# A hybrid encoder layer on eight cores: projections, GpSimd sums, output tiles and first loads rearranged

## The chip, the cores and the metric

The kernel runs on the 8 cores of one Trainium2 chip. Each core computes its own slice of the batch and exchanges nothing with the others; all read the same weights from HBM. A time is the device time of the slowest core, in microseconds (us). TensorE (PE) multiplies; VectorE (DVE), ScalarE (ACT) and GpSimd (POOL) work elementwise; SyncE (SP) only issues DMAs, and GpSimd issues those that convert float32 to bfloat16 on the way.

## The reference

One layer, applied to 4 prompts of 4096 tokens and 16 samples of 32 tokens, with 1024 features:

```
x = x + 0.5 * SwiGLU_1(RMSNorm(x))                     # 1024 -> 2 x 2816 -> 1024
h = RMSNorm(x)
u, q, k, v, ga, gb = split(h @ w_in)                   # 512 | 1024 | 128 | 128 | 1024 | 1024
q, k = RMSNorm per head;  16 heads of 64, 2 KV heads
A = (pool(u, windows 2/4/8/16) - u) @ w_group * scale + bias ... @ w_pool_proj
B = attention over the own 64-token chunk and two before, with sinks ... @ w_attn_proj
x = x + (sigmoid(ga) * A + sigmoid(gb) * B) @ w_out
x = x + 0.5 * SwiGLU_2(RMSNorm(x))
```

It also returns the last pooling inputs (`o_pool_p`, `o_pool_s`) and the last K and V rows.

## The kernel before, in words

A core has 2240 token columns: 128 of halo, 2048 of a prompt, 64 of two samples. They lie in 5 groups `X[0]`..`X[4]` of 448 columns, features on partitions, as 8 tiles (kc or m) of 128 features. Group 0 has only 320 columns after the first feed-forward, since the halo falls away. `hT` holds the normed activations in bf16, for matmuls. Nearly all matmuls are 128x128 by 448 columns. In the profiled names `ring` is a buffer of 7 weight blocks, which GpSimd's queue fills from `wst` (`pump`); a block is loaded when an earlier one is released.

The instruction order on every engine is the order of the Python calls: `Prog` puts each operation on its engine's list and adds the semaphore waits that its reads and writes ask for. A DMA takes the next of its queue's semaphores (12 for SP, 12 for GpSimd), and so waits until the DMA 12 before it on that queue has landed. `P.guard()` is the last operation so far on each compute engine; an operation with `extra=mguard` waits for these.

Stages, with the core's times in the profile:

- **First feed-forward** (0 to 537). A norm is `norm_sq`: ScalarE squares tile kc of a group, TensorE adds the eight squares over the partitions with a matmul by a constant (L448), `norm_fin` takes ln and exp on ScalarE (L457, L459) into one of two `rstd` buffers, and VectorE multiplies X by it into `hT` (L462); these eight products wait in `hq`, and `drain(k)` issues k of them. `lagq` holds the constant matmuls; `tick(k)` issues all but the last k. `gate_multi` multiplies hidden blocks j for one group (L505); two blocks at once are interleaved kc by kc. `first_pass1` orders the first four blocks, during the loads. `out_proj` (L566) adds the result to X on VectorE (L570), and in its last pass also squares for the next norm, n2.
- **Projections** (537 to 657). For g in 0..4, `seq` calls K, V, the pool inputs U(0..3) and the queries Q(0..7). Each is followed by `next_step`, which drains products and issues the later parts of earlier steps: K and Q need `stat_mm` (a constant matmul L676 into the one bank 7, then ln and exp L678/L680 into an `rstd` buffer), U(c) has window sums on GpSimd (c + 1 adds, L750 to L757) and then a VectorE product into `ya` (L791). `kT`, `Vb` and the sample tiles `ksT`, `Vs` are cleared by GpSimd first (L621, L622, L848). V's copy (L727) carries `mguard`.
- **Attention with branch A** (657 to 797). 32 attention units, each scores (L923), exp, values (L966), a normed output in a tile `yt` (L986), and a DMA transpose of that tile into `qT` on SP's queue (L991). There are two such tiles in turn. Between them run gate (L1010) and projection (L1023) of branch A; the product into `mT[g]` (L1028) overwrites memory of X, `ub`, `ktm` and `vtm`. For the samples, `u_fin` sums and `u_last` finishes `ya`.
- **Branch B** (797 to 912), then **the mix output** (912 to 977): 5 groups x 8 tiles of 8 matmuls (L1106), X on VectorE (L1108), squares (L444) and constant matmuls (L448) for the norm n3.
- **Second feed-forward** (977 to the end), whose last pass sends X to `y_out` two tiles at a time.

## Time and profile before

| | us |
|---|---|
| median of 3 runs (1451.29 to 1614.0) | 1452.57 |
| the profiled execution | 1451.66 |
| its span, first to last instruction, slowest core (core 0) | 1450.6 |
| the other cores' spans | 1445.1 to 1449.7 |
| granted TensorE clock, every core | 1.000 |
| TensorE busy in the span | 1419.3 |
| VectorE, ScalarE, GpSimd busy | 608.4, 391.4, 139.3 |

The span is what the trace shows; the profiled execution's own time is 1.06 us more, for what lies before the first and behind the last instruction. Busy time of TensorE is the union of its matmuls, so a matmul that overlaps the one before it counts once. The "idle before" of an instruction is in square brackets in the timeline, with what ended it.

### The profile page before, as it was taken

To read this page: it belongs to the slowest core of one execution; us is meant where nothing else is said; L and a number is where in the kernel's file an instruction comes from. 1 tells how busy PE (TensorE), PEld (TensorE's weight loads), DVE (VectorE), ACT (ScalarE), POOL (GpSimd) and SP (SyncE) were. 2 spreads that over 40 slices of the span, in tenths; PEclk is the share of its full clock that TensorE was granted. 3 is DMA by queue.
4 is the path that set the end of the run, shared out by engine and by line. 5 is a ranking of instruction groups with operands and counts; after the bars stand their busy time and mean duration, and the time that the engine had idled before them with its cause. 6 is when DMAs were issued, how large, how long until landed. Compare 5 with 4: busy or idle time off the path is not lost.

```text
span 1450.6 us, 23849 instructions; the slowest of 8 cores (1445.1 to 1450.6 us)
## 1 busy us (share of the span) xinstructions
PE 1419.3 (98%) x8189; PEld 777.2 (54%) x8189; DVE 608.4 (42%) x1159; ACT 391.4 (27%) x640; POOL 139.3 (10%) x214
## 2 busy tenths in 40 slices
PE   5999999999999999998999999999999999999999
PEld 2555555555555455555666555555555555555554
DVE  3436226223422485565555344563252251253235
ACT  5620110111011356556554222442101101101110
POOL 2010000000000045561000000000000000000000
PEclk9999999999999999999999999999999999999999
DMA  9743410321011341226434812224404204200014
GB/s 227 173 66 49 72 31 15 51 52 30 1 30 30 93 191 27 25 31 106 67 67 59 247 30 44 66 47 78 79 2 73 45 1 73 45 1 1 1 37 203
DMA packets 61172, 93.04 MB, mean 64 GB/s; under 512 B 42912, under 2 KB 44512, under 8 KB 59776
## 3 DMA queue, kind: packets, MB, share of 16 engines
q0 software_dynamic: 17936, 57.32, 22.4%
q1 hardware_dynamic: 43120, 34.20, 8.0%
q8 instruction: 69, 1.13, 0.3%
q14 instruction: 47, 0.39, 0.1%
HBM read 114.97 MB, written 18.38 MB: 92 GB/s over the span
## 4 chain that ended last, share of the span: by engine, by line
PE 89%; DMA 3%; SPq 2%; issue 2%; DVE 2%; POOL 1%; ACT 1%; DVEq 0%; POOLq 0%; ACTq 0%
PE ps L505 44%; PE ps L566 22%; PE ps L1085 4%; PE ps L1090 4%; PE ps L1106 4%; PE ps L1010 2%; PE ps L836 2%; DMA qT<-yt 2%; PE ps L448 1%; PE ps L771 1%; PE ps L1023 1%; PE ps L923 1%; PE ps L966 1%; SPq L700 1%; DMA X<-xin 1%
## 5 line engine op out<-in xcount | busy, mean ns | idle before, releaser
L505 PE MATMUL ps<-hT,ring 128*128 128x448 bf16 (+1 forms) x3520 | 651.1, 348 | 4.2 <-DVE hT L462 3.9
L505 PEld LDWEIGHTS ps<-hT,ring 128*128 128x128 bf16 x3520 | 344.5, 98 | 308.8 <-issue 7.8
L519 DVE TENSOR_TENSOR Abuf<-ps,sl 128x448 bf16<-128x448 f32 (+1 forms) x220 | 134.0, 611 | 481.1 <-PE ps L505 463.8
L566 PE MATMUL ps<-Abuf,Wo 128*128 128x448 bf16 (+1 forms) x1760 | 330.9, 347 | 0.0
L518 ACT ACTIVATE sl<-ps 128x448 bf16<-128x448 f32 (+1 forms) x220 | 116.7, 533 | 727.1 <-PE ps L505 720.2
L566 PEld LDWEIGHTS ps<-Abuf,Wo 128*128 128x128 bf16 x1760 | 172.2, 98 | 151.1
L570 DVE SCALAR_TENSOR_TENSOR X<-ps,X 128x448 f32<-128x448 f32 (+1 forms) x320 | 195.5, 611 | 114.9 <-PE ps L566 113.4
L394 POOL DMA_DIRECT2D ring<-wst x71 | 38.2, 539 | 903.6 <-PE ps L505 608.3
L462 DVE SCALAR_TENSOR_TENSOR hT<-X,colv,rstd 128x448 bf16<-128x448 f32 (+1 forms) x120 | 76.6, 669 | 37.9 <-ACT rstd L459 37.9
L1010 PE MATMUL ps<-hT,ring 128*128 128x448 bf16 (+1 forms) x320 | 63.7, 342 | 0.1
L1085 PE MATMUL ps<-hT,ring 128*128 128x448 bf16 (+1 forms) x320 | 63.6, 342 | 0.0
L1090 PE MATMUL ps<-qT,ring 128*128 128x448 bf16 (+1 forms) x320 | 63.6, 342 | 0.0
L1106 PE MATMUL ps<-mT,ring 128*128 128x448 bf16 (+1 forms) x320 | 63.1, 342 | 0.0
L444 ACT ACTIVATE sq<-X 128x448 bf16<-128x448 f32 (+1 forms) x80 | 45.2, 565 | 64.7 <-DVE X L1108 37.8
L836 PE MATMUL ps<-hT,ring 128*128 128x448 bf16 (+1 forms) x320 | 61.5, 342 | 0.0
L929 ACT ACTIVATE PT<-ps,colv 128x1536 bf16<-128x1536 f32 (+2 forms) x34 | 49.8, 1466 | 42.3 <-DVE yt L986 24.4
L1092 DVE SCALAR_TENSOR_TENSOR pb<-tb,ps 128x448 f32<-128x448 f32 (+1 forms) x40 | 23.8, 595 | 63.0 <-PE ps L1090 61.3
L1087 ACT ACTIVATE tb<-ps,hbg 128x448 f32<-128x448 f32 (+1 forms) x40 | 24.5, 613 | 89.0 <-DVE mT L1094 55.1
L1085 PEld LDWEIGHTS ps<-hT,ring 128*128 128x128 bf16 x320 | 31.3, 98 | 25.8
L1090 PEld LDWEIGHTS ps<-qT,ring 128*128 128x128 bf16 x320 | 31.3, 98 | 25.8
L1106 PEld LDWEIGHTS ps<-mT,ring 128*128 128x128 bf16 x320 | 31.3, 98 | 25.7
L836 PEld LDWEIGHTS ps<-hT,ring 128*128 128x128 bf16 x320 | 31.1, 98 | 25.6 <-issue 0.3
(104 smaller groups left out, 803.4 us busy)
## 6 DMA issues: line engine op xcount, KB each, us to landing
ring<-wst POOLq DMA_DIRECT2D x63, 512.0 KB, 6.3
Wo<-wo POOLq DMA_DIRECT2D x12, 768.0 KB, 9.9
xsp<-X SPq DMA_DIRECT2D x5, 1792.0 KB, 6.1
X<-xsp SPq DMA_DIRECT2D x5, 1792.0 KB, 17.6
X<-xin POOLq DMA_DIRECT2D x8, 896.0 KB, 29.9
y_out<-X SPq DMA_DIRECT2D x6, 896.0 KB, 3.6
ring<-wst POOLq DMA_DIRECT2D x8, 384.0 KB, 10.0
Wo<-wo POOLq DMA_DIRECT2D x4, 512.0 KB, 5.6
```

The lines of the kernel that those rows point to most:

```text
L462: P.dve(lambda: V.scalar_tensor_tensor(out=hT[:, kc, C0[g] + lo:C0[g] + lo + n], in0=X[g][:, kc, lo:lo + n], scalar=cv_[:, gcol + kc:gcol ...
L505: P.pe(lambda: T.matmul(ps[:, bks[x][half], 0:n], lhsT=w[:, kc, 128 * half:128 * half + 128], rhs=hT[:, kc, c0s[g]:c0s[g] + n], start=(kc ...
L518: P.act(lambda: S.activation(out=slt[i][:, 0:n], in_=ps[:, bg, 0:n], func=AF.Silu), r=[bank[bg]], w=[r_sl[i]])
L519: P.dve(lambda: V.tensor_tensor(out=Abuf[:, jj, c0s[g]:c0s[g] + n], in0=ps[:, bu, 0:n], in1=slt[i][:, 0:n], op=ALU.mult), r=[bank[bu], r_s ...
L566: P.pe(lambda: T.matmul(ps[:, bk, 0:n], lhsT=Wo[b][:, jj, 128 * m:128 * m + 128], rhs=Abuf[:, jj, c0s[g]:c0s[g] + n], start=(jj == 0), sto ...
L570: P.dve(lambda: V.scalar_tensor_tensor(out=X[g][:, m, lo[g]:lo[g] + n], in0=ps[:, bk, 0:n], scalar=0.5, in1=X[g][:, m, lo[g]:lo[g] + n], o ...
L836: P.pe(lambda: T.matmul(ps[:, bk, 0:n], lhsT=w[:, kc, 128 * (m % 2):128 * (m % 2) + 128], rhs=hT[:, kc, c0:c0 + n], start=(kc == 0), stop= ...
L929: P.act(lambda: S.activation(out=pt[:, a:z, :], in_=ps[:, a:z, :], func=AF.Exp, scale=0.125, bias=cv_[:, col:col + 1]), r=[bank[x] for x i ...
L1010: P.pe(lambda: T.matmul(ps[:, gb, 0:n], lhsT=w[:, kc, :], rhs=hT[:, kc, c0:c0 + n], start=(kc == 0), stop=(kc == KC - 1)), r=rw + [rh[g][k ...
L1085: P.pe(lambda: T.matmul(ps[:, bg, 0:n], lhsT=w[:, kc, :], rhs=hT[:, kc, c0:c0 + n], start=(kc == 0), stop=(kc == KC - 1)), r=rw + [rh[g][k ...
L1090: P.pe(lambda: T.matmul(ps[:, bp, 0:n], lhsT=w[:, 8 + x, :], rhs=qT[:, mm0 // 64:(mm0 + n) // 64, x, :], start=(x == 0), stop=(x == 7)), r ...
L1106: P.pe(lambda: T.matmul(ps[:, bk, 0:n], lhsT=w[:, c, 128 * (m % 2):128 * (m % 2) + 128], rhs=mT[g][:, c, :], start=(c == 0), stop=(c == 7) ...
```

## The change

- SP's queue gets 24 DMA semaphores. Group 0's four load pieces go from GpSimd's queue to SP's. GpSimd's weight loads wait for the first of the pieces.
- `first_pass1` runs blocks 0 and 1 of group 0 together and finishes group 0's four blocks before group 1's.
- In the last pass of `out_proj` before a norm, the drain behind tile 4 is left out. The last group's n2 norm has an `rstd` buffer of its own, `rst2`. `next_step` drains one product instead of two. Group 0's pool inputs are taken in the order 0, 1, 2, 3.
- For n3, GpSimd adds the squares of tiles 0 to 6 (six adds a group, into `accL` and at last into a bf16 tile), and TensorE runs two constant matmuls a group instead of eight, behind the first output tile of the next group.
- The pooling outputs go from SP's queue to GpSimd's. The loads into `ksT` and `Vs` have a resource for each half. `yt` gets a third tile. `u_last` of 3 and 2 moves into the last group's last two steps, that of 1 and 0 behind the first `mT` product.
- The last output tile of the last group is computed and sent in two halves of 224 columns, tile 6 by itself.

```diff
+    accB, e = at("accB", [128, GW], BF16, mend)
+    e = scr + NSQ * 2 * GW
+    accL, e = at("accL", [128, GW], F32, e)
+    accM, e = at("accM", [128, GW], BF16, e)
...
-    P = Prog(nc)
+    P = Prog(nc, {"sp": 24, "pool": 12})
...
-    yts, r_yts = [yt, yt2], [R("yt"), R("yt2")]
+    yts, r_yts = [yt, yt2, yt3], [R("yt"), R("yt2"), R("yt3")]
+    al_y = [r_sq[2:4], [], r_rst[1:2]]
...
+    r_us, r_kn = R("usT"), R("kns")
+    r_ks, r_vs = [R("ksT0"), R("ksT1")], [R("Vs0"), R("Vs1")]
...
-            P.dma("pool", lambda: nc.gpsimd.dma_start(out=ring[:, 2048 * sl_:2048 * sl_ + w_], in_=wst[i, :, 0:w_]), w=[r_ring[sl_]])
+            P.dma("pool", lambda: nc.gpsimd.dma_start(out=ring[:, 2048 * sl_:2048 * sl_ + w_], in_=wst[i, :, 0:w_]), w=[r_ring[sl_]], extra=x0[0:1])
...
-    load_x(0, 2)
+    x0 = [P.dma("sp", lambda a=a: nc.sync.dma_start(out=X[0][:, a:a + 2, :], in_=xin[:, 0, a:a + 2, :]), w=rX[0][a:a + 2])
+          for a in range(0, KC, 2)]
     pump_to(2)
     load_x(1, 4)
     pump_to(4)
...
-        lagq.append(mm)
+        if key != "n3":
+            lagq.append(mm)
+            return
+        ac, rac = accL, r_sl[0:2]
+        ab, rab = (accB, r_accB) if g % 2 == 0 else (accM, r_sl[2])
+        if kc == 0:
+            sqp[g] = (t, rt)
+        elif kc < KC - 1:
+            src, rsrc = (sqp[g][0], [sqp[g][1]]) if kc == 1 else (ac, rac)
+            dst, rdst = (ab, [rab]) if kc == KC - 2 else (ac, rac)
+            P.gps(lambda: G.tensor_tensor(out=dst[:, 0:n], in0=src[:, 0:n], in1=t[:, 0:n], op=ALU.add), r=rsrc + [rt], w=rdst,
+                  extra=ng_["sq"])
+        else:
+            def mm2():
+                P.pe(lambda: T.matmul(ps[:, sbk, 0:n], lhsT=cb[:, 0, :], rhs=ab[:, 0:n], start=True, stop=False),
+                     r=[rab, r_cb], w=[bank[sbk]])
+                P.pe(lambda: T.matmul(ps[:, sbk, 0:n], lhsT=cb[:, 0, :], rhs=t[:, 0:n], start=False, stop=True),
+                     r=[rt, r_cb], w=[bank[sbk]])
+                norm_fin(key, g, lo, n, gcol, sbk)
+            lagq.append(mm2)
...
+        if key == "n2" and g == NG - 1:
+            rs, rrs = rst2, r_rst2
+        else:
+            i = cnt["rst"] % 2
+            cnt["rst"] += 1
+            rs, rrs = rst[i], r_rst[i]
...
             feed(0)
             tick(0)
             drain(8)
-            gate_multi([(0, 0)], 0, True)
+            post = gate_multi([(0, 0), (1, 1)], 0, post=False)
             feed(1)
-            post = gate_multi([(1, 1)], 0, post=False)
             tick(0)
-            drain(8)
+            drain(3)
             post()
+            drain(3)
             gate_multi([(2, 2)], 0)
-            feed(2)
-            gate_multi([(0, 0), (1, 1)], 1)
-            gate_multi([(2, 2)], 1)
+            drain(2)
             gate_multi([(3, 3)], 0)
-            tick(0)
-            drain(8)
...
             for m in range(KC):
                 bk = nb(FB6 if last and gcol_next is not None else FB)
-                for jj in range(len(js)):
-                    P.pe(lambda: T.matmul(ps[:, bk, 0:n], lhsT=Wo[b][:, jj, 128 * m:128 * m + 128],
-                                          rhs=Abuf[:, jj, c0s[g]:c0s[g] + n], start=(jj == 0), stop=(jj == len(js) - 1)),
-                         r=[r_Wo[b], r_A[jj][g]], w=[bank[bk]], sig=(jj == len(js) - 1))
+                end = last and store and g == NG - 1 and m == KC - 1
                 rx_ = [rX[g][m]]
-                P.dve(lambda: V.scalar_tensor_tensor(out=X[g][:, m, lo[g]:lo[g] + n], in0=ps[:, bk, 0:n], scalar=0.5,
-                                                     in1=X[g][:, m, lo[g]:lo[g] + n], op0=ALU.mult, op1=ALU.add),
-                      r=[bank[bk]] + rx_, w=rx_)
-                drain(1)
+                for (a, z) in ([(0, n // 2), (n // 2, n)] if end else [(0, n)]):
+                    if a:
+                        bk = nb(FB)
+                    for jj in range(len(js)):
+                        P.pe(lambda: T.matmul(ps[:, bk, 0:z - a], lhsT=Wo[b][:, jj, 128 * m:128 * m + 128],
+                                              rhs=Abuf[:, jj, c0s[g] + a:c0s[g] + z], start=(jj == 0), stop=(jj == len(js) - 1)),
+                             r=[r_Wo[b], r_A[jj][g]], w=[bank[bk]], sig=(jj == len(js) - 1))
+                    wx_ = [R("end%d" % a)] if end else rx_
+                    P.dve(lambda: V.scalar_tensor_tensor(out=X[g][:, m, lo[g] + a:lo[g] + z], in0=ps[:, bk, 0:z - a], scalar=0.5,
+                                                         in1=X[g][:, m, lo[g] + a:lo[g] + z], op0=ALU.mult, op1=ALU.add),
+                          r=[bank[bk]] + rx_, w=wx_)
+                    if end:
+                        out_dmas.append(P.dma("sp", lambda: nc.sync.dma_start(
+                            out=y_out[:, g, m:m + 1, lo[g] + a:lo[g] + z], in_=X[g][:, m:m + 1, lo[g] + a:lo[g] + z]), r=wx_))
+                if not (last and gcol_next is not None and m == 4):
+                    drain(1)
                 if last and gcol_next is not None:
                     norm_sq(next_key, g, m, lo[g], n, gcol_next)
                 tick(2)
                 if last and store:
-                    step = 2 if g == NG - 1 else 4
-                    if m % step == step - 1:
+                    step = 4 if g < NG - 1 else 2 if m < 6 else 1
+                    if m % step == step - 1 and not end:
                         a = m - step + 1
                         out_dmas.append(P.dma("sp", lambda a=a, m=m, g=g: nc.sync.dma_start(
...
         sched["t"] += 1
         tick(0)
-        drain(2)
+        drain(1)
...
         if cg == 3:
-            out_dmas.append(P.dma("sp", lambda: nc.sync.dma_start(out=o_pool_p, in_=b[:, :, o - 16:o]), r=rbs))
-            out_dmas.append(P.dma("sp", lambda: nc.sync.dma_start(out=o_pool_s, in_=b[:, :, o:o + 64]), r=rbs))
+            out_dmas.append(P.dma("pool", lambda: nc.gpsimd.dma_start(out=o_pool_p, in_=b[:, :, o - 16:o]), r=rbs))
+            out_dmas.append(P.dma("pool", lambda: nc.gpsimd.dma_start(out=o_pool_s, in_=b[:, :, o:o + 64]), r=rbs))
...
         for p in range(2):
             P.dma("pool", lambda p=p: nc.gpsimd.dma_start(
-                out=ksT[64 * p:64 * p + 64, :, :, :, p, :].rearrange("k s h c q -> k (s h c) q"), in_=ckT), w=[r_ks])
+                out=ksT[64 * p:64 * p + 64, :, :, :, p, :].rearrange("k s h c q -> k (s h c) q"), in_=ckT), w=[r_ks[p]])
             P.dma("pool", lambda p=p: nc.gpsimd.dma_start(
-                out=Vs[64 * p:64 * p + 64, :, :, :, p, 0:64].rearrange("k s c h d -> k (s c h) d"), in_=cvT), w=[r_vs])
+                out=Vs[64 * p:64 * p + 64, :, :, :, p, 0:64].rearrange("k s c h d -> k (s c h) d"), in_=cvT), w=[r_vs[p]])
...
-        def Q(m, yc=None, uf=None):
+        def Q(m, yc=None, uf=None, ul=None):
             def f():
+                if ul is not None:
+                    u_last[ul]()
...
-        if g < NG - 1:
+        if g == 0:
+            seq = [K, Vv(0, 1, 2, 3), U(0), Q(0), Q(1), U(1), Q(2, 3), Q(3), U(2), Q(4, 2), Q(5), U(3), Q(6, 1), Q(7, 0)]
+        elif g < NG - 1:
             seq = [K, Vv(0, 1, 2, 3), U(3), Q(0), Q(1), U(2), Q(2, 3), Q(3), U(1), Q(4, 2), Q(5), U(0), Q(6, 1), Q(7, 0)]
         else:
-            seq = [U(3), K, U(2), Vv(0, 1, 2, 3), U(1), Q(0), U(0), Q(1, None, 3), Q(2, 3, 2), Q(3, 2, 1), Q(4, 1, 0), Q(5, 0), Q(6), Q(7)]
+            seq = [U(3), K, U(2), Vv(0, 1, 2, 3), U(1), Q(0), U(0), Q(1, None, 3), Q(2, 3, 2), Q(3, 2, 1), Q(4, 1, 0), Q(5, 0), Q(6, None, None, 3), Q(7, None, None, 2)]
...
-        k = ucnt["y"] % 2
+        k = ucnt["y"] % 3
         ucnt["y"] += 1
         yo, ryo = yts[k], r_yts[k]
         for h in range(2):
...
-                  r=[bank[3 + h], r_dn2[h]], w=[ryo] + ([] if k else al_yt))
+                  r=[bank[3 + h], r_dn2[h]], w=[ryo] + al_y[k])
...
-    turn = [[], [(3, 4), (2, 1)], [(1, 4), (0, 3)]]
+    turn = [[], [(3, 4), (2, 6)], [(1, 4), (0, 3)]]
...
+            a_mul(c, g, pbn)
             if ai == 0:
-                for x in (3, 2, 1, 0):
-                    u_last[x]()
-            a_mul(c, g, pbn)
+                u_last[1]()
+                u_last[0]()
             if ai < len(turn):
...
             drain(1)
+            tick(0)
             norm_sq("n3", g, m, lo_, n, C_G3)
-            tick(2)
```

How the change moves instructions at three places. Names: `X_44` to `X_48` are groups 0 to 4, `mT_120`/`mT_125` is group 0's mix input and `mT_86`/`mT_87` group 1's, `vtm` V's copy, `ub` a pool input, `ktm` K's result, `sq` a tile of squares, `cb` the constants; rows give line, operation, tiles, size, and how often in a row.

VectorE, from the last output tiles of the first feed-forward into the first projections, before:

```order
L462 SCALAR_TENSOR_TENSOR hT<-X_47,colv,rstd_64 128x448
L570 SCALAR_TENSOR_TENSOR X_48<-ps,X_48 128x448
L462 SCALAR_TENSOR_TENSOR hT<-X_47,colv,rstd_64 128x448 x3
L462 SCALAR_TENSOR_TENSOR hT<-X_48,colv,rstd_64 128x448 x2
L727 CAST vtm_97<-ps 128x384
L729 CAST vtm_97<-ps 64x128
L462 SCALAR_TENSOR_TENSOR hT<-X_48,colv,rstd_64 128x448 x2
L775 COPY ub_95<-ps 128x336
L462 SCALAR_TENSOR_TENSOR hT<-X_48,colv,rstd_64 128x448 x2
L696 SCALAR_TENSOR_TENSOR ktm_96<-ps,colv,rstd_65 128x448
```

and now:

```order
L607 SCALAR_TENSOR_TENSOR X_48<-ps,X_48 128x448 x2
L499 SCALAR_TENSOR_TENSOR hT<-X_46,colv,rstd_65 128x448
L607 SCALAR_TENSOR_TENSOR X_48<-ps,X_48 128x448
L499 SCALAR_TENSOR_TENSOR hT<-X_47,colv,rstd_64 128x448
L607 SCALAR_TENSOR_TENSOR X_48<-ps,X_48 128x448
L499 SCALAR_TENSOR_TENSOR hT<-X_47,colv,rstd_64 128x448 x7
L499 SCALAR_TENSOR_TENSOR hT<-X_48,colv,rst_101 128x448
L768 CAST vtm_98<-ps 128x384
L770 CAST vtm_98<-ps 64x128
L499 SCALAR_TENSOR_TENSOR hT<-X_48,colv,rst_101 128x448
L816 COPY ub_96<-ps 128x336
```

Seven products of group 3 stand behind the last output tile where three stood, and the last product of group 2 stands two output tiles from the end, where it stood six from it; those of group 4 come one at a time.

TensorE, the first groups of the mix output, before:

```order
L1106 MATMUL ps<-mT_120,ring 128x320 x24
L448 MATMUL ps<-sq_57,cb 128x320
L1106 MATMUL ps<-mT_120,ring 128x320 x8
L448 MATMUL ps<-sq_58,cb 128x320
L1106 MATMUL ps<-mT_120,ring 128x320 x8
L448 MATMUL ps<-sq_59,cb 128x320
```

and now:

```order
L1151 MATMUL ps<-mT_125,ring 128x320 x64
L1151 MATMUL ps<-mT_87,ring 128x448 x8
L480 MATMUL ps<-accB,cb 128x320
L482 MATMUL ps<-sq_60,cb 128x320
L1151 MATMUL ps<-mT_87,ring 128x448 x56
```

A constant matmul stood behind every output tile; now two stand behind the first tile of the next group, of which the first reads what GpSimd's last add wrote.

GpSimd's queue at the start, before:

```order
L381 DMA X_44<-xin 128x896 x4
L394 DMA ring<-wst 128x2048 x2
L381 DMA X_45<-xin 128x1792 x2
L394 DMA ring<-wst 128x2048 x2
L381 DMA X_46<-xin 128x1792 x2
```

and now:

```order
L406 DMA ring<-wst 128x2048 x2
L393 DMA X_45<-xin 128x1792 x2
L406 DMA ring<-wst 128x2048 x2
L393 DMA X_46<-xin 128x1792 x2
L393 DMA X_47<-xin 128x1792 x2
```

The four pieces of group 0 left this queue; the rest kept its order.

## Rows read from the trace of the kernel before

**Rows 1.** The page's head and part 1, busy time by engine, its first line.

```profile
span 1450.6 us, 23849 instructions; the slowest of 8 cores (1445.1 to 1450.6 us)
...
PE 1419.3 (98%) x8189; PEld 777.2 (54%) x8189; DVE 608.4 (42%) x1159; ACT 391.4 (27%) x640; POOL 139.3 (10%) x214
```

**Rows 2.** Busy time by stretch: length, then each engine's, clock, DMA share, GB/s.

```profile
0.00:60.00 60.00, 43.76 (x204) 20.14 (x205) 21.25 (x40) 34.14 (x57) 11.77 (x25) 1.00 0.91 221
...
480.00:540.00 60.00, 59.15 (x329) 31.00 (x327) 44.00 (x74) 30.12 (x52) 16.60 (x5) 1.00 0.38 144
540.00:600.00 60.00, 55.25 (x370) 32.60 (x368) 32.96 (x60) 35.42 (x69) 34.28 (x49) 1.00 0.28 47
...
660.00:800.00 140.00, 134.19 (x1091) 89.40 (x1090) 73.85 (x260) 76.31 (x80) 5.18 (x12) 1.00 0.44 71
...
914.00:978.00 64.00, 64.00 (x360) 35.04 (x359) 40.12 (x69) 28.82 (x51) 2.83 (x5) 1.00 0.26 62
```

**Rows 3.** Timeline of the start: start, duration, engine, line, operation, [idle before].

```profile
1.06 0.40 SPq L377 DMA_DIRECT2D colv<-colv  x1
...
1.57 2.30 POOL L381 DMA_DIRECT2D X<-xin  x4 [0.87 <-POOLq L158]
...
13.62 1.04 ACT L444 ACTIVATE sqx<-X 128x448 bf16<-128x448 f32 x2 [1.15 <-DMA X<-xin]
...
16.67 0.53 POOL L394 DMA_DIRECT2D ring<-wst  x1 [2.06 <-DMA ring<-wst]
...
17.92 7.63 PE L505 MATMUL ps<-hT,ring 128*128 128x448 bf16 x32 [2.58 <-DVE hT L462]
...
19.88 0.71 POOL L492 DMA_DIRECT2D Wo<-wo  x1 [2.67 <-DMA ring<-wst]
...
36.58 1.98 ACT L444 ACTIVATE sqx<-X 128x448 bf16<-128x448 f32 x4 [0.34 <-DMA X<-xin]
...
50.23 6.21 PE L505 MATMUL ps<-hT,ring 128*128 128x448 bf16 x32 [0.65 <-DVE hT L462]
```

**Rows 4.** DMA issues of the page: count, KB each, median us to landing.

```profile
y_out<-X SPq DMA_DIRECT2D x4, 448.0 KB, 2.5
...
colv<-colv SPq DMA_DIRECT2D x1, 80.0 KB, 2.0
```

**Rows 5.** Timeline of the projections' start and of the sample set-up.

```profile
530.39 7.69 POOL L622 MEMSET Vb<- 128x9100 bf16 x1 [3.02 <-ACT sq L444]
...
538.19 0.93 POOL L624 MEMSET Vb<- 64x70 bf16 x2
...
542.05 0.55 DVE L727 CAST vtm<-ps 128x384 bf16<-128x384 f32 x1
...
544.52 1.27 DVE L462 SCALAR_TENSOR_TENSOR hT<-X,colv,rstd 128x448 bf16<-128x448 f32 x2
...
544.81 1.58 POOL L750 TENSOR_TENSOR S<-ub 128x335 f32<-128x335 f32 x1 [5.68 <-DVE ub L775]
...
547.15 0.30 PE L676 MATMUL ps<-sq,cb 128*128 128x320 bf16 x1 [1.51 <-ACT rstd L678]
...
550.61 0.87 DVE L791 SCALAR_TENSOR_TENSOR ya<-S,ub 128x320 bf16<-128x320 f32 x1 [2.62 <-POOL S L789]
...
591.12 0.68 POOL L857 DMA_DIRECT2D ksT<-ckT  x1 [3.52 <-DMA Vs<-cvT]
```

**Rows 6.** Timeline of the attention's start.

```profile
662.92 0.35 PE L825 MATMUL ps<-ya,Wpw 128*128 128x448 bf16 x1 [1.32 <-DVE mT L1028]
...
673.16 0.62 DVE L1028 SCALAR_TENSOR_TENSOR mT<-tg,ps 128x448 bf16<-128x448 f32 x1 [5.44 <-DMA o_pool_s<-ub]
```

**Rows 7.** Groups by shape: GpSimd's adds; VectorE's products within 914 to 978.

```profile
L753 POOL TENSOR_TENSOR S<-S 128x461 f32<-128x461 f32 x9 | 8.6, 955 | 1.3
...
L462 DVE SCALAR_TENSOR_TENSOR hT<-X,colv,rstd 128x448 bf16<-128x448 f32 x22 | 14.9, 677 | 0.7 <-ACT rstd L459 0.7
```

**Rows 8.** Timeline of one square in the mix output, and of the last output tile.

```profile
929.35 0.58 ACT L444 ACTIVATE sq<-X 128x448 bf16<-128x448 f32 x1 [0.90 <-DVE X L1108]
...
1447.19 0.62 DVE L570 SCALAR_TENSOR_TENSOR X<-ps,X 128x448 f32<-128x448 f32 x1 [0.51 <-PE ps L566]
```

43 lines of the change are left out of this document (23 added, 20 removed).

## Prediction

> **What bounds the kernel now.** I read the views in this order. The page's first part: TensorE is busy in 1419.3 of 1450.6 us, and no other engine in half of it [rows 1]. So there are two ways to gain: matmuls that go away, and the 31.3 us in which TensorE idles. The table of stretches says where these are: 16.2 us in the first 60, 0.9 in 480 to 540, 4.8 in 540 to 600, 5.8 in 660 to 800; what is left, 3.6 us, lies behind the last matmul [rows 2]. Everywhere else TensorE is full, and work of other engines is free as long as nobody waits for it. The timeline of each such stretch then names the wait [rows 3, 5, 6]. A 448-column matmul costs (6.21 - 0.16) / 32 = 0.189 us (32 in 6.21, of which 0.16 is the last one's overlap) [rows 3]; one of 320 columns 320/448 of it, 0.135.
>
> The sum is made against the profiled execution, 1451.66 us; the median shown is 0.9 us higher.
>
> **Start.** Today group 0's last piece is squared at 13.62, TensorE's first gate matmul runs 4.3 us later, at 17.92, weight blocks 0 and 1 have landed at 16.67 and 19.88 (GpSimd waits for them to reuse their semaphores), and the second half of group 2 at 36.58 [rows 3]. From 13.62 to 36.58 landed four blocks (128 x 2048 x 4 bytes, 1.05 MB each) and two groups (1.84 MB each), 7.87 MB in 23.0 us, 343 KB/us. Group 0's four blocks in the new order need the same amount: groups 0 and 1, blocks 0 to 3. A DMA of SP issued at 1.06 landed 2.0 us later [rows 3, 4], so the stream runs from about 3.1, and I add 1.0 for the hold, in which SP's pieces run alone: block 3 lands at 3.1 + 23.0 + 1.0 = 27.1. Behind it stand its 16 matmuls (3.0) and, for group 1, 32 gate matmuls, 8 constant ones and 32 more (13.6): group 2's first gate matmul at 43.7, today 50.23 [rows 3]. **-6.5 us.** The pairing itself gives four matmuls per product of VectorE (0.76 against 0.61 us), where two were not enough, but the landing covers this. Ends: if SP's pieces come no faster than GpSimd's did, the stream is only shifted by the queue's earlier first byte, about 1.5 us: block 3 at 13.6 + 6.03/0.343 - 1.5 = 29.7, so -3.9. If only TensorE counted, group 0 landing at 8.5 (3.1 + 1.84/0.343), first matmul at 12.8, then 144 matmuls (27.2): 40.0, -10. The row on the rate is the nearest to both, so I stay with the value in between.
>
> The Trainium skill ("DMA: Bandwidth & Descriptors", Issuing engines are not separate DMA queues) says that all queues share the same 16 DMA engines, so another queue gives no more bandwidth. By it the gain is in the first byte alone, the -3.9 end. No row here shows both queues loading at once at the start.
>
> **Last pass before n2, and projections.** Today TensorE waits 1.5 us at 547.15 and 1.8 at 552.70 for an `rstd` buffer; behind the first stands VectorE, whose product of K comes late behind pairs of group 4's products, behind the second VectorE again, held 2.62 us by GpSimd's chain for U(3), which is slowed to 1.58 us for a 335-column add beside VectorE's products [rows 5]. `rst2`, one drain a step and U(0) first (one add) take both causes away. But the skipped drains leave seven products of group 3 for the end, and the last product of group 2 now comes four output tiles later (4 x 1.33 us). GpSimd's clearing of `Vb` writes over group 2 and waits for it: it began at 530.39 and ended, with the two small ones, at 539.1 [rows 5]; it will end at about 544.3. V's copy carries `mguard` and ran at 542.05 [rows 5], so VectorE's queue now stands until 544.3. Behind it: copies 0.9, product 0.6, copy 0.5, product 0.6, K's product 0.6, and so on to the first query's product at 550.7; that query's `rstd` buffer is needed for the third query's ln, and the fourth's constant matmul, wanted at 549.5, waits for bank 7 until about 551.3. I put 1.9 us of wait in the place of 3.3: **-1.4**. Ends: 0 and -3.3, as the wait for the clearing is covered or not.
>
> At 591.12 GpSimd had waited 3.52 us for the first half of `Vs` before it could issue the second, and the window sums behind it came late; of that 1.4 us reached TensorE (4.75 in 540 to 600, less the two above) [rows 2, 5]. With a resource per half the wait is gone: **-1.4**, nothing late behind it.
>
> **Attention.** At 673.16 VectorE had stood 5.44 us for `o_pool_s`, issued last on a congested SP queue; TensorE lost 2.2 of it. At 662.92 TensorE waited 1.3 us for bank 1 behind eight small `ya` products [rows 6]. On GpSimd's queue the two outputs are issued near 651, behind two weight loads, and have until 669 to land; they push GpSimd's sample sums by about 1.4 us (two issues of 0.7, as the one at 591.12 [rows 5]), which VectorE's slack there takes. -2.2, and -0.8 for the bank, since `mT`, the last four `ya` products and bank 4 still come in a row. The other 2.2 us of the stretch [rows 2] are spread over six places where `yt` waits for the transpose that reads it; a third tile adds a unit's time, 3.6 us, and I take 1.9 of it. Sum **-4.9**, ends -2.5 (the pooling outputs land late behind the weight loads) and -5.8.
>
> **Mix output.** The stretch 914 to 978 is full [rows 2]. Six constant matmuls a group go: 4 x 6 x 0.189 + 6 x 0.135 = -5.3 us. What is put in: six GpSimd adds a group, one per output tile (8 x 0.189 = 1.51 us). An f32 add of 461 columns takes 0.955 [rows 7], 448 columns 0.93. Beside VectorE it is slower: the 335-column add would take 0.73 by columns and took 1.58, while about 1.1 us of products ran [rows 5], so it lost 0.75 of the overlap. A product takes 0.68 in each 1.51 [rows 7]: add 0.93 + 0.75 x 0.68 = 1.43, with a gap of 0.13 it is 1.56 a tile. From the end of tile 1's matmuls: X 0.62 and square 0.58 [rows 8] and three hand-overs of some 0.15 give 1.65; six adds end at 1.65 + 5 x 1.56 + 1.43 = 10.9. TensorE wants the sum behind tile 0 of the next group, seven tiles later, at 10.6. So 0.4 us of wait with the hand-over, in four groups (the fifth has 16 matmuls of the next stage as cover): +1.5. Net **-3.8**, ends -5.3 (the adds keep 0.93) and -0.1 (next paragraph). The fewer matmuls make the tile 1.51 instead of 1.70 us; VectorE needs 1.30 of it.
>
> The Trainium skill ("SBUF — State Buffer", Who interferes with whom) says that a VectorE instruction with two SBUF inputs and a GpSimd instruction that reads SBUF exclude each other wholly. The row shows three quarters of the overlap lost, not all.
>
> **Tail.** The last X operation starts at 1447.19, takes 0.62, and its DMA of 448 KB lands about 2.5 later [rows 4, 8]. A half tile takes some 0.39 on VectorE and 112 KB land nearer to the 2.0 of the small load [rows 4]: **-0.7**, ends -0.2 and -1.2. The 0.9 us in 480 to 540 stay.
>
> Sum: -6.5 - 1.4 - 1.4 - 4.9 - 3.8 - 0.7 = -18.7, so 1433.0 us.
>
> **Rivals.**
> - *The adds are fully locked out.* Then an add is 0.93 + 0.68 = 1.61, with the gap 1.74 a tile; six end at 1.65 + 8.7 + 1.61 + 0.1 = 12.1, 1.5 us late in three groups beside full-width products, 0.9 in the one beside 320-column ones: +5.4 in place of +1.5, 1437 us. For it: the adds are slowed at all; against: the 1.58. This is what the skill's rule would do.
> - *The start gains only the first byte*: -3.9 in place of -6.5, 1435.5 us. With the lock-out as well, 1439.5.
> - *The clearing of `Vb` and the late outputs cost what they were to save*: projections at -1.4 together, attention at -2.5: 1437 us.
> - *Slower than before.* The sum on GpSimd becomes TensorE's bound. The adds read bf16, and no row has an add of two bf16 tiles. With a us a tile, a sum is 6a - 8.8 late; the other gains and the matmuls make 20.2 us, so over four groups it turns at 6a = 13.9, a = 2.3 us, 2.4 times today's 0.955. At 2.5 us: 1451.7 - 20.2 + 4 x 6.2 = 1456. Against: the slowest 335-column row scales to 2.1 us at 448 columns, and there products ran for 70% of the time.
> - *It does not do what it says*: the third tile or the early transfer changes nothing, as SP's congestion between 650 and 670 stays; that is inside the ends above.
>
> **Chances and range.** A measurement of this kernel tells about 2% (29 us) from no change. The forecast with its terms near their values, 1428 to 1436: 0.55. Rivals that leave 1436 to 1441, alone or two together: 0.27. Better than 1428, more terms at their good ends (all of them give 1425): 0.10. Above 1441: 0.08, of it 0.03 above 1452. Range 1427 to 1441. Over 2% faster means under 1423.5, beyond all good ends together: 0.02. Over 2% slower asks for adds of 3.5 us: 0.02. Within 2%: 0.96.
>
> **What would show it.** Group 2's first gate matmul at 43 to 45 us; blocks 0 and 1 landed by 16. A VectorE wait of about 2 us before V's copy, released by the clearing of `Vb`, and one wait of about 2 us of TensorE before 552. No GpSimd wait in the sample set-up. No wait of `mT` for `o_pool_s`, no wait of `yt` for a transpose. In the mix output, GpSimd adds of 1.3 to 1.5 us and waits of under 0.6 us before four of the new constant matmuls. The forecast is wrong if these adds take over 1.7 us, or if the landing of the first blocks is not earlier than today.

## The result and the profile after

The changed kernel takes 1435.49 us (median of 1435.44 to 1435.60), the kernel before took 1451.29 and 1452.57: a ratio of 0.9884, interval 0.9865 to 0.9904. Executions in which the cores of a die ran long at a lower granted clock are left out, here and in every time below. The forecast was 1433.0, the range 1427 to 1441. The total held; how it is made up did not.

The page's head and its first line of busy time, after:

```profile
span 1434.4 us, 23887 instructions; the slowest of 8 cores (1432.7 to 1434.4 us)
...
PE 1413.2 (99%) x8165; PEld 775.7 (54%) x8165; DVE 616.3 (43%) x1160; ACT 388.6 (27%) x638; POOL 168.9 (12%) x242
```

Against [rows 1] TensorE now idles 21.2 us, not 31.3. The stretches that answer to [rows 2] (length, then each engine's busy time, clock, DMA share, GB/s):

```profile
0.00:60.00 60.00, 45.53 (x211) 21.48 (x212) 21.53 (x41) 32.68 (x57) 9.55 (x21) 1.00 0.90 221
540.00:600.00 60.00, 58.06 (x378) 33.88 (x376) 35.63 (x65) 37.17 (x71) 41.21 (x56) 1.00 0.26 38
660.00:800.00 140.00, 139.12 (x1125) 93.15 (x1126) 74.88 (x256) 75.83 (x81) 5.15 (x12) 1.00 0.49 81
914.00:978.00 64.00, 63.98 (x347) 33.74 (x346) 52.17 (x76) 29.71 (x50) 27.85 (x29) 1.00 0.29 61
```

The idle time of 540 to 800 is nearly gone; that of the start (14.5 us) is not. VectorE is 12 us busier in the last stretch, but that stretch now holds 18 us of the second feed-forward. In the mix output by itself VectorE is busy 48.0 us, before 40.7 (core 0), with one product a tile as before. These 7 us will matter below.

Idle time in a window says little once the windows hold different work. So I cut both traces at the same matmuls (the first output matmul, the first of the projections, the first gate matmul of branch A, the first of branch B, of the mix output, of the second feed-forward, and the last) and took the median of the eight cores for each piece, in us:

| piece | before | after | measured | forecast |
|---|---|---|---|---|
| start to first output matmul | 104.71 | 102.57 | -2.1 | -6.5 |
| projections | 118.78 | 117.02 | -1.8 | -2.8 |
| attention with branch A | 138.28 | 134.30 | -4.0 | -4.9 |
| branch B | 114.24 | 114.24 | 0 | 0 |
| mix output | 63.88 | 58.96 | -4.9 | -3.8 |
| behind the last matmul | 4.02 | 2.98 | -1.0 | -0.7 |

(The rest of the two feed-forwards takes 432.1 and 471.4 us before, 432.1 and 471.5 after.) These make 13.8 us, while the slowest core's span fell by 16.2. The difference is spread among the cores: attention took 136.8 to 140.4 us on the eight cores before and takes 134.3 to 134.5 now, and the time is that of the slowest core. Core 0, the slowest before, won 2.3, 2.9, 6.1, 0, 4.9 and 0.9 us in the six rows.

### The profile page after: what moved, and what is told of

Same layout as the page of the kernel before. It is cut to its first block, busy times and chain, and to the rows that moved or that the text cites. A ratio compares the mean times of both kernels' runs of the same rounds, so it can differ in the third digit from the quotient of the medians.

```text
span 1434.4 us, 23887 instructions; the slowest of 8 cores (1432.7 to 1434.4 us)
## 1 busy us (share of the span) xinstructions
PE 1413.2 (99%) x8165; PEld 775.7 (54%) x8165; DVE 616.3 (43%) x1160; ACT 388.6 (27%) x638; POOL 168.9 (12%) x242
## 4 chain that ended last, share of the span: by engine, by line
PE 98%; DMA 1%; issue 0%; DVE 0%; ACT 0%; POOL 0%; SPq 0%; DVEq 0%; ACTq 0%; POOLq 0%
PE ps L542 45%; PE ps L603 22%; PE ps L1055 4%; PE ps L1151 4%; PE ps L1135 4%; PE ps L1130 4%; PE ps L877 4%; PE ps L1068 2%; PE ps L812 2%; PE ps L1011 1%; PE ps L968 1%; PE ps L462 1%; DMA ring<-wst 1%; PE ps L763 1%; PE ps L717 1%; PE ps L731 1%
## 5 line engine op out<-in xcount | busy, mean ns | idle before, releaser
L603 PE MATMUL ps<-Abuf,Wo 128*128 128x448 bf16 (+2 forms) x1766 | 330.9, 346 | 0.0
L499 DVE SCALAR_TENSOR_TENSOR hT<-X,colv,rstd 128x448 bf16<-128x448 f32 (+1 forms) x112 | 79.5, 739 | 34.0 <-ACT rstd L496 34.0
L458 ACT ACTIVATE sq<-X 128x448 bf16<-128x448 f32 (+1 forms) x80 | 45.0, 564 | 57.6 <-DVE X L1153 30.7
L1151 PE MATMUL ps<-mT,ring 128*128 128x448 bf16 (+1 forms) x320 | 57.9, 342 | 0.0
L877 PEld LDWEIGHTS ps<-hT,ring 128*128 128x128 bf16 x320 | 31.1, 98 | 26.6 <-issue 1.2
L1135 PEld LDWEIGHTS ps<-qT,ring 128*128 128x128 bf16 x320 | 31.3, 98 | 25.8
L1130 PEld LDWEIGHTS ps<-hT,ring 128*128 128x128 bf16 x320 | 31.3, 98 | 25.8
L1151 PEld LDWEIGHTS ps<-mT,ring 128*128 128x128 bf16 x320 | 31.3, 98 | 25.2
```

The lines of the kernel that those rows point to most:

```text
L499: P.dve(lambda: V.scalar_tensor_tensor(out=hT[:, kc, C0[g] + lo:C0[g] + lo + n], in0=X[g][:, kc, lo:lo + n], scalar=cv_[:, gcol + kc:gcol ...
L603: P.pe(lambda: T.matmul(ps[:, bk, 0:z - a], lhsT=Wo[b][:, jj, 128 * m:128 * m + 128], rhs=Abuf[:, jj, c0s[g] + a:c0s[g] + z], start=(jj == ...
L877: P.pe(lambda: T.matmul(ps[:, bk, 0:n], lhsT=w[:, kc, 128 * (m % 2):128 * (m % 2) + 128], rhs=hT[:, kc, c0:c0 + n], start=(kc == 0), stop= ...
L1130: P.pe(lambda: T.matmul(ps[:, bg, 0:n], lhsT=w[:, kc, :], rhs=hT[:, kc, c0:c0 + n], start=(kc == 0), stop=(kc == KC - 1)), r=rw + [rh[g][k ...
L1135: P.pe(lambda: T.matmul(ps[:, bp, 0:n], lhsT=w[:, 8 + x, :], rhs=qT[:, mm0 // 64:(mm0 + n) // 64, x, :], start=(x == 0), stop=(x == 7)), r ...
L1151: P.pe(lambda: T.matmul(ps[:, bk, 0:n], lhsT=w[:, c, 128 * (m % 2):128 * (m % 2) + 128], rhs=mT[g][:, c, :], start=(c == 0), stop=(c == 7) ...
```

## The experiments

All are edits of the changed kernel, each compared on the same chip with the kernel before.

### The start

Its timeline after (start, duration, engine, line, operation, idle before and what ended it), against [rows 3]:

```profile
7.32 1.21 POOL L406 DMA_DIRECT2D ring<-wst  x2 [6.61 <-DMA X<-xin]
...
12.50 1.04 ACT L458 ACTIVATE sqx<-X 128x448 bf16<-128x448 f32 x2 [1.27 <-DMA X<-xin]
...
16.71 0.53 POOL L406 DMA_DIRECT2D ring<-wst  x1 [2.90 <-DMA ring<-wst]
16.80 0.90 PE L542 MATMUL ps<-hT,ring 128*128 128x448 bf16 x2 [2.58 <-DVE hT L499]
19.28 8.64 PE L542 MATMUL ps<-hT,ring 128*128 128x448 bf16 x30 [1.58 <-DMA ring<-wst]
...
27.76 1.68 PE L462 MATMUL ps<-sqx,cb 128*128 128x448 bf16 x8
...
29.27 12.27 PE L542 MATMUL ps<-hT,ring 128*128 128x448 bf16 x64
...
42.89 12.27 PE L542 MATMUL ps<-hT,ring 128*128 128x448 bf16 x64
```

Group 0's last piece comes 1.1 us earlier, blocks 0 and 1 no earlier at all. TensorE stops after two matmuls for block 1. Then 30 matmuls take 8.64 us: one by one, the first 15 of them start 0.373 us apart, the rest 0.189. 448 columns in 0.373 us are 1.2 GHz, the lower of the two levels, though the granted clock reads 1.00 in this stretch; ahead of them TensorE had run for 0.9 us in the last 5. On core 0 of the kernel before 8 gate matmuls were so slow; over the cores it is 8 to 16 before and 11 to 16 now. Group 2's first gate matmul is the 33rd of the last row, at 48.9 (48.1 on the median core), where 43.7 was forecast.

From 19.28 on TensorE has no pause in these rows. Block 3's first matmul is the 17th of the row at 29.27, at 32.3, while block 3 landed at 30.7. So it is on all eight cores: block 3's first matmul starts 0.5 to 1.6 us behind its landing, with no wait for it. What TensorE does wait for is block 1, 1.3 to 2.3 us.

**Undo the start, and undo the queue alone.** Both put group 0 back on GpSimd's queue; the first also restores the old order of blocks.

```diff
-    x0 = [P.dma("sp", lambda a=a: nc.sync.dma_start(out=X[0][:, a:a + 2, :], ...
+    load_x(0, 2)
...
-..., w=[r_ring[sl_]], extra=x0[0:1])
+..., w=[r_ring[sl_]])
```

> The changed kernel with its start undone: group 0's pieces on GpSimd's queue again, no hold, and the old order of the first blocks. My reading of the two traces: the start is worth the 2.3 us by which core 0's projections begin earlier, so 1437.9 us, group 2's first gate matmul back at 50.2 and that of the changed kernel at 48 to 49. The prediction's own term was 6.5: then 1442. If the start is worth nothing, 1435.6.

> The changed kernel with group 0's pieces on GpSimd's queue and no hold, but with the new order of the first blocks. From the start to the first output matmul lie 102.6 us in the changed kernel, 104.7 with the old start. If the order is what counts: 102.6 to 103, and SP's queue is worth little; if SP's queue is (its last piece lands 1.1 us earlier): 103.7 to 104, the end 1437.

Measured: 1439.12 us with the old start, 1437.06 with the new order on the old queue. The first piece of the kernel lasts 104.69 and 102.92 us, against 102.57. So the order of blocks is worth 1.8 us. The 0.35 of SP's queue can't be told from nothing: seven executions with the changed kernel's start (it, its repetition and five runs below that change later stages) gave 102.0 to 102.9 us for this piece. With SP's queue the first gate matmul starts 1.1 us earlier, at 16.2 for 17.3; TensorE then waits longer for block 1 (1.66 us for 1.02) and runs 14.5 slow matmuls in place of 12.5 (all medians), and the 1.1 us are spent. Both runs lost 0.8 us more in the mix output, 59.8 us for 59.0, on all cores, with not one instruction changed there; see below.

**Without the hold.**

```diff
-..., w=[r_ring[sl_]], extra=x0[0:1])
+..., w=[r_ring[sl_]])
```

> The changed kernel without GpSimd's wait for the first piece of group 0. Theory H (the hold cost the stream what SP's queue gained: block 3 landed at 30.74, before at 30.77): without it blocks 0 to 3 land 2.5 to 3.5 us earlier, the 1.6 us wait for block 1 goes, fewer gate matmuls run 0.373 us apart, and the end comes 2 to 3 us earlier, 1433 us. Rival (the two queues only share, and group 0's pieces are what TensorE needs first): the last piece lands 1.5 to 3 us later, the first gate matmul with it at 18.5 or later, blocks no use before: 1435.5 to 1437.

Measured: 1442.97 us, 7.5 slower than the changed kernel; the first piece takes 109.4 us, 6.8 more. Blocks 0 and 1 do land earlier, as the first theory has it (block 3 doesn't), and group 0 later, as the second has it, but by 9.6 us and not by 1.5 to 3; the first gate matmul starts at 25.7. The squares of group 0 in that run:

```profile
7.10 1.04 ACT L458 ACTIVATE sqx<-X 128x448 bf16<-128x448 f32 x2 [1.10 <-DMA X<-xin]
...
12.82 1.04 ACT L458 ACTIVATE sqx<-X 128x448 bf16<-128x448 f32 x2 [4.68 <-DMA X<-xin]
...
17.77 1.04 ACT L458 ACTIVATE sqx<-X 128x448 bf16<-128x448 f32 x2 [3.90 <-DMA X<-xin]
...
22.25 1.04 ACT L458 ACTIVATE sqx<-X 128x448 bf16<-128x448 f32 x2 [3.44 <-DMA X<-xin]
...
26.55 9.06 PE L542 MATMUL ps<-hT,ring 128*128 128x448 bf16 x32 [2.58 <-DVE hT L499]
```

Beside GpSimd's stream SP's pieces land 4 to 6 us apart; with GpSimd held until the first had landed they came 1.5 to 2.3 apart. Landings in us, medians of the cores:

| | group 0, last piece | block 0 | block 1 | block 3 |
|---|---|---|---|---|
| before | 12.9 | 16.0 | 18.9 | 30.7 |
| old start | 12.9 | 16.0 | 18.9 | 31.3 |
| new order, old queue | 13.0 | 16.0 | 19.1 | 30.9 |
| changed | 11.8 | 15.8 | 18.7 | 30.5 |
| without the hold | 21.4 | 11.5 | 16.1 | 31.1 |

Block 3 lands at 30.5 to 31.3 whatever the queue, the hold and the order of the first pieces. The forecast had 27.1. Why no order of these loads brings it earlier was not tested.

**Blocks 0 and 1 one after the other.**

```diff
-            post = gate_multi([(0, 0), (1, 1)], 0, post=False)
+            gate_multi([(0, 0)], 0, True)
             feed(1)
+            post = gate_multi([(1, 1)], 0, post=False)
```

> The changed kernel with blocks 0 and 1 of group 0 one after the other instead of interleaved. Theory P: the pairing made TensorE wait 1.6 us for block 1 at 17.7 and start again with slow matmuls, 17 at 0.373 us in place of 8; without it both go, 3 us on TensorE, of which blocks 2 and 3 (27.8 and 30.7) leave about 1: 1434.5 us. Rival: VectorE's products (0.61 us each for two matmuls) stretch the first block again and nothing is won: 1435.5.

Measured: 1435.33 us (1434.83 to 1435.53), first piece 102.08 us. The wait for block 1 is gone, and 10 matmuls are slow, not 14.5 (medians); but 102.08 lies within the 102.0 to 102.9 of equal starts, and the whole time tells nothing either.

**Zero matmuls to keep the clock up**, alone and with the blocks apart. `warm(k)` issues k matmuls of a cleared 448-column tile.

```diff
             feed(0)
-            tick(0)
+            warm(16)
+            for k in (6, 4, 8, 14):
+                tick(len(lagq) - 2)
+                warm(k)
             drain(8)
```

> The changed kernel with 48 extra matmuls of zeros on TensorE before the first gate matmul (16 ahead of the first constant one, then 6, 4, 8 and 14 behind its pairs), so that TensorE hardly idles between 2.5 and 16 us. Theory C: the 17 gate matmuls that ran 0.373 us apart ran at 1.2 GHz because TensorE had idled, and run 0.19 us apart here, worth 3.2 us on TensorE; as block 3 lands at 30.7 only 1.5 to 2 of them reach the end: 1433.8 us. Rival: the 0.373 comes from the late data or from the loads' traffic, not from the clock: the spacing stays, 1435.5.

> The changed kernel with blocks 0 and 1 one after the other and zero matmuls wherever TensorE would idle before 27 us (48 ahead of the first gate matmul, 20 ahead of group 1's constants). The landings (block 2 near 27.9, block 3 near 30.7) stay. Theory L (the landings bound the start, the slow matmuls and the wait for block 1 hide in front of them): block 3's matmuls end at 34.3 in place of 35, the first output matmul at 101.5 to 102 (102.1 with the blocks alone), the end at 1434.8 to 1435.3 us. Rival (the slow matmuls reach the end): 100.5 and 1433.7.

Measured: 1436.07 us alone, 1437.91 with both (and 20 zero matmuls ahead of group 1's constants). TensorE in the first of these runs, core 0:

```profile
16.82 0.54 PE L543 MATMUL ps<-hT,ring 128*128 128x448 bf16 x2
...
19.05 5.84 PE L543 MATMUL ps<-hT,ring 128*128 128x448 bf16 x30 [1.69 <-DMA ring<-wst]
...
26.40 1.75 PE L463 MATMUL ps<-sqx,cb 128*128 128x448 bf16 x4 [0.76 <-ACT sqx L459]
...
28.50 7.71 PE L543 MATMUL ps<-hT,ring 128*128 128x448 bf16 x31 [0.35 <-DMA ring<-wst]
```

The clock theory holds: 30 matmuls take 5.84 us, not 8.64, with the same loads under way. And it is worth nothing (first piece 102.75 us): TensorE then waits for group 1's squares and block 2, and after that nine matmuls are 0.373 apart again. Five of the eight cores have seven to nine such slow matmuls, three of them already behind the wait for block 1; three cores have none. The length of the pauses doesn't sort them: core 4 has none behind pauses of 2.26 and 1.60 us, core 3 has seven behind one of 1.85. With the long filler no core has a slow matmul, and TensorE pauses for 0.34 us in all between its first gate matmul and group 2's; it is no faster, since 20 x 0.189 = 3.8 us of zeros stand where the waits and the slow matmuls were (first piece 103.4 us). The slowest cores of that run also ended 5 us behind their last matmul, where 3 is usual; that is the larger part of its 1437.9 and I have no cause for it. The changed kernel run beside it took 1435.45.

> The changed kernel itself on the same chip, for the comparison: 1435.5 us.

**Block 2 ahead of group 1, and its queue mended.** The loads go W0, W1, W2, group 1, W3, and group 0's three blocks run before group 1's constants.

```diff
-    pump_to(2)
+    pump_to(3)
     load_x(1, 4)
...
             drain(8)
-            post = gate_multi([(0, 0), (1, 1)], 0, post=False)
+            gate_multi([(0, 0)], 0, True)
+            gate_multi([(1, 1)], 0, True)
+            post = gate_multi([(2, 2)], 0, True, post=False)
             feed(1)
             tick(0)
-            drain(3)
             post()
-            drain(3)
-            gate_multi([(2, 2)], 0)
-            drain(2)
+            drain(8)
             gate_multi([(3, 3)], 0)
```

The first of the two runs has zero matmuls besides.

> The changed kernel with block 2 loaded ahead of group 1 (landing some 21.5 us instead of 27.8), blocks 0, 1 and 2 of group 0 one after the other, then group 1's constant matmuls, then block 3, and with zero matmuls (48 ahead of the first gate matmul, 10 ahead of group 1's constants) so that TensorE's clock stays up. Blocks 0 to 3 of group 0 end when block 3 has landed (30.7) plus its 16 matmuls, at 33.7 instead of 35.3 to 36: first output matmul at 100 to 101 in place of 102.6, the end 1433.5 us. If group 1's pieces, now 2.5 us later, hold it up: 102.6, 1435.5.

> The same without the zero matmuls. If the slow gate matmuls hide behind the landing of block 3, as in the run with zero matmuls alone, this is as fast as its sister: 1433.5 us; if not, 1.5 us slower.

Measured: 1439.22 and 1438.71 us, first piece 105.5 and 104.8. VectorE's products of group 1 stood behind block 2's product, and that behind ScalarE's table loads (1.28 us each); TensorE idled 2.0 to 3.0 us ahead of group 1's first gate matmul, near 36. The second version puts `post()` between the halves of group 1's squares:

> As best_w, but block 2's silu between the two halves of group 1's squares and its product ahead of group 1's eight, since there VectorE's products stood behind that product and ScalarE's table loads (first gate matmul of group 1 at 35.8 us, 2 to 3 us of idle ahead of it). If that queue was all that was wrong, group 1's gates start at 33.5 to 34, the first output matmul comes at 101 to 101.5 (102.6 in the changed kernel), and the end at 1434 us. If the landings (block 2 at 21.6, group 1 at 27.2) leave nothing to win, 102.6 and 1435.5.

> The same without the zero matmuls: equal to its sister if the slow matmuls fit in the time until block 3 lands, 1434 us; 1435 if not.

Measured: 1436.06 and 1435.90 us, first piece 102.5 and 102.8.

**One piece of group 0 on SP's queue, the other three first on GpSimd's**, without the hold and with blocks 0 and 1 apart, then with the order just told:

> Only the first piece of group 0 on SP's queue, the other three first on GpSimd's, no hold, blocks 0 and 1 one after the other. Theory S (a queue's own start and the hold, not the bandwidth, set when the stream runs: in the changed kernel block 0 landed 3.8 us after group 0's last piece, before 2.6): the last piece lands at 11.5 to 12.5, block 0 near 14.5, block 1 near 17.5, block 3 near 29.5, the first output matmul at 101 to 101.5 us, the end at 1434. Rival (the sharing of the two queues delays the pieces, as without the hold, where the first gate matmul came at 25.7): first gate matmul after 17.5 and 1436 us or more.

> x_one's loads with b3_n's order of blocks: if both help, the first output matmul at 100 us and the end at 1433 us; if TensorE, and not the stream, is the bound by then, as x_one.

Measured: 1436.40 and 1437.07 us, first piece 102.55 and 103.4. Apart from the two with the blocked queue, the start of every variant with a new order of blocks and group 0 not starved lasts 102.1 to 103.4 us, and most of that is the spread of equal starts.

### The sums on GpSimd

```diff
-        if key != "n3":
+        if True:
             lagq.append(mm)
             return
...
-            tick(0)
             norm_sq("n3", g, m, lo_, n, C_G3)
+            tick(2)
```

> The changed kernel with the sums of n3 back on TensorE: eight constant matmuls a group, no GpSimd adds. Between the first matmul of the mix output and the first gate matmul of the second feed-forward lie 59.0 us in the changed kernel and 63.9 in the one before. Theory A (only the matmuls count, 24 x 0.189 + 6 x 0.135 = 5.3 us, less some waits): 63.9 us here, the end 4.9 later, 1440.4. The prediction's 3.8 would give 1439.3. Second theory, on who pays where both engines read SBUF: VectorE's products of this stage took 0.68 us before and 0.85 with the adds at 1.03; without the adds they take 0.68 again.

Measured: 1440.32 us; the mix output takes 63.88 us, as before. So the sums on GpSimd are worth 4.9 us, close to the 5.3 of the matmuls taken out; no wait came in their place. Groups by shape (count, busy, mean ns of one, idle before) of the changed kernel, GpSimd's adds on core 5 (895 to 978) and VectorE's products on core 0 (905 to 978, so some of the next stage's are among them):

```profile
L476 POOL TENSOR_TENSOR accL<-accL,sq 128x448 f32<-128x448 f32 x16 | 16.6, 1038 | 7.3 <-ACT sq L458 6.3 <-PE ps L1151 0.9
```

```profile
L499 DVE SCALAR_TENSOR_TENSOR hT<-X,colv,rstd 128x448 bf16<-128x448 f32 x32 | 26.9, 854 | 1.4 <-ACT rstd L496 1.4
```

and of the kernel with the sums on TensorE, core 0, the same stretch:

```profile
L499 DVE SCALAR_TENSOR_TENSOR hT<-X,colv,rstd 128x448 bf16<-128x448 f32 x32 | 21.3, 677 | 1.9 <-ACT rstd L496 1.9
```

The adds keep 1.04 us. It is VectorE's product that pays: 0.854 in place of 0.677, 5.6 us over these 32, all of it in slack. The forecast had GpSimd pay, at 1.43 an add.

Which of the two pays goes by which starts first. Group 1's first add in the changed kernel, core 0:

```profile
914.29 1.03 POOL L476 TENSOR_TENSOR accL<-sq,sq 128x448 f32<-128x448 bf16 x1 [4.26 <-ACT sq L458]
914.36 1.30 DVE L499 SCALAR_TENSOR_TENSOR hT<-X,colv,rstd 128x320 bf16<-128x320 f32 x1
```

and the same in the kernel with the old start, core 0, where everything up to here lies 3.50 us later:

```profile
917.86 0.54 DVE L498 SCALAR_TENSOR_TENSOR hT<-X,colv,rstd 128x320 bf16<-128x320 f32 x1
918.09 1.20 POOL L475 TENSOR_TENSOR accL<-sq,sq 128x448 f32<-128x448 bf16 x1 [4.56 <-ACT sq L457]
...
919.43 5.91 POOL L475 TENSOR_TENSOR accL<-accL,sq 128x448 f32<-128x448 f32 x4
925.49 1.37 POOL L475 TENSOR_TENSOR accM<-accL,sq 128x448 bf16<-128x448 f32 x1
```

Here the product starts 0.23 us ahead of the add and takes its 0.54; the add takes 1.20. From then on that chain of adds runs without a pause at 1.37 each, 1.5 apart, each behind a product's start, and TensorE waits 0.7 us for the sum. In the changed kernel the add started 0.07 us ahead, kept 1.03, and the product took 1.30. All cores agree. Take the pairs of a full-width add and a product that start within 0.4 us of each other, with no earlier add beside the product. In the changed kernel the add is first in all 24 of them: it keeps its 1.03 to within 0.01, and the product takes 0.48 to 0.76 us more. With the old start the product is first in 48 of 56: it keeps its 0.54, and the add takes 0.17 to 0.35 us more; in the other eight it is as in the changed kernel. The kernel with the new order on GpSimd's queue shows the same 48. So 0.3 us of start decide over 0.8 us of the end; what delayed the add in these two kernels the traces don't show. The Trainium skill ("SBUF — State Buffer", Who interferes with whom) says, of VectorE's two-port modes, that whoever issues first gets the shared ports for the whole instruction. The order agrees; but locked out wholly, the product would have taken 0.96 + 0.54 = 1.50, and it took 1.30.

**Every add twice.**

```diff
+            P.gps(lambda: G.tensor_tensor(out=ab[:, 0:n], in0=src[:, 0:n], in1=t[:, 0:n], op=ALU.add), ...
             P.gps(lambda: G.tensor_tensor(out=dst[:, 0:n], in0=src[:, 0:n], in1=t[:, 0:n], op=ALU.add), ...
```

> The changed kernel in which GpSimd does every add of the n3 sum twice, the extra one into the bf16 tile: 12 a group. By the prediction's formula a sum of six is 6a - 8.8 us late with a us a tile; with a = 2 x 1.04 = 2.1 that is 3.7 us in three groups and 0.7 in the first, 12 us in all: 1447.5 us, and more, up to 1456, if the adds then lie beside VectorE's products all the time and GpSimd is the one that is held up (a = 2.5). If VectorE pays instead, its products grow over 0.85 and the adds stay at 1.04: 1447.

Measured: 1475.17 us, 1.6% slower than the kernel before. TensorE's waits between 900 and 1000 (in total, times, longest), and its clock (third column from the end) by stretch, core 0, where the mix output lasts from 899.8 to 990.8:

```profile
PE ps L482 <- POOL accB L478: 16.5, 3, 7.1
PE ps L482 <- POOL accM L478: 12.6, 2, 6.6
```

```profile
900.00:930.00 30.00, 24.04 (x138) 13.61 (x136) 14.97 (x27) 10.54 (x19) 19.64 (x21) 0.94 0.27 80
930.00:960.00 30.00, 17.79 (x77) 8.47 (x78) 10.68 (x17) 7.39 (x13) 18.90 (x17) 0.74 0.00 1
...
992.00:1000.00 8.00, 3.00 (x16) 1.65 (x14) 1.44 (x3) 3.02 (x4) 7.41 (x9) 0.74 0.11 11
1000.00:1010.00 10.00, 10.00 (x51) 5.29 (x50) 6.59 (x11) 4.38 (x7) 0.76 (x2) 0.87 1.05 179
1010.00:1020.00 10.00, 10.00 (x55) 5.19 (x53) 1.87 (x3) 1.74 (x4) 0.56 (x1) 1.00 0.71 106
```

With 12 adds of about 1.2 us the queue never empties. By the prediction's formula a sum 6.6 us late means (6.6 + 8.8) / 6 = 2.6 us a tile. So the slower rival is real. At 2.6 us a tile its formula gives 4 x 6.6 = 26 us of waits in four groups; measured on core 0 are 24.1. Two things come on top. The fifth group waits too, 5.0 us, which the forecast held covered; this wait lies already in the next stage. And TensorE's clock falls once it pauses in every group: the granted clock has a mean of 0.74 in two of the stretches, between the levels of 1.2 and 2.4 GHz, and 38 matmuls of the mix output are 0.373 us apart, which costs about 7 us (some 9 on cores 3 and 5). The mix output takes 31.9 us more, the stage after it, of which not one instruction is changed, 7.7: the fifth wait and 1.4 to 2.0 us of slow matmuls. The point from which the rival decides was not tested more closely.

### Attention

```diff
-            out_dmas.append(P.dma("pool", lambda: nc.gpsimd.dma_start(out=o_pool_p, ...
+            out_dmas.append(P.dma("sp", lambda: nc.sync.dma_start(out=o_pool_p, ...
```

> The changed kernel with the two pooling outputs back on SP's queue. Attention takes 134.3 us on every core of the changed kernel, and 136.8 to 140.4 before. Theory O (the wait of mT for o_pool_s on SP is what made the cores differ): cores between 135.5 and 138, the end by the worst of them, 1438 us. Rival (the third yt tile takes SP's queue out of the chain, so that the output lands in time there too): 1435.6.

```diff
-    yts, r_yts = [yt, yt2, yt3], [R("yt"), R("yt2"), R("yt3")]
+    yts, r_yts = [yt, yt2], [R("yt"), R("yt2")]
...
-        k = ucnt["y"] % 3
+        k = ucnt["y"] % 2
```

> The changed kernel with two yt tiles in turn in place of three. The prediction gives the third tile 1.9 us: attention 136.2 us in place of 134.3, 1437.4 us. Rival (the waits of yt for a transpose came with the congestion by the outputs, which is gone): 134.3 to 134.8, 1435.6 to 1436.

Measured: 1438.24 us with the outputs on SP (attention 135.3 to 138.0 over the cores, median 136.7), 1442.28 with two tiles (135.8 to 140.4, median 138.8). The waits of VectorE (total, times, longest), outputs on SP, core 1:

```profile
DVE mT L1073 <- DMA o_pool_s<-ub: 5.7, 1, 5.7
```

two tiles, core 2:

```profile
DVE yt L1031 <- DMA qT<-yt: 10.5, 7, 4.8
```

Neither is in the changed kernel. The two don't add: of the 4.0 us, the third tile alone brings 138.3 - 136.7 = 1.6, the outputs alone 138.3 - 138.8, less than nothing. In the changed kernel a transpose lands 3.6 us after its issue (median of 32), before 2.5, and four reloads of X fall into the same stretch, before two:

```profile
X<-xsp SPq DMA_DIRECT2D x4, 1792.0 KB, 22.2
...
qT<-yt SPq DMA_TRANSPOSE x32, 3.6
```

With the outputs away from SP's queue its transposes land later, beside earlier reloads, and only a third tile covers that. That the reloads are the reason was not tested, nor were the moves of `u_last` undone: TensorE's wait of 1.3 us behind the `ya` products (L825 before) is still 0.7 long (L866, core 5).

### Projections

```diff
-        drain(1)
+        drain(2)
...
-                if not (last and gcol_next is not None and m == 4):
-                    drain(1)
+                drain(1)
...
-        if key == "n2" and g == NG - 1:
+        if False:
```

(and group 0's pool inputs in the order 3, 2, 1, 0)

> The changed kernel with the drains, the last group's rstd buffer and the order of group 0's pool inputs as before; what stays of the change to the projections is the resource per half of ksT and Vs. Projections take 117.0 us in the changed kernel and 118.8 before (medians of the eight cores). By the prediction the two parts are worth 1.4 us each: 118.4 here. If the whole gain is the halves': 117.0, and the drains did nothing.

Measured: projections 118.2 us, in place of 117.0 and 118.8. The drains with `rst2` and the order are worth 1.2. The 0.6 that are left I put down to the halves of `ksT` and `Vs`, which were not undone by themselves. (The whole took 1435.82 and 1436.59 us in two executions.) The new wait stands where it was forecast, in the changed kernel:

```profile
543.22 0.56 DVE L768 CAST vtm<-ps 128x384 bf16<-128x384 f32 x1 [2.25 <-POOL Vb L665]
...
546.51 1.25 PE L877 MATMUL ps<-hT,ring 128*128 128x320 bf16 x8 [0.94 <-DVE ktm L737]
```

## Why the prediction was right or wrong

- **Start: wrong**, -2.1 for -6.5. The failed step is the landing of block 3 at 27.1, and with it the remark that the landing covers what TensorE loses ahead of it. The step took 343 KB/us, read between 13.62 and 36.58, for the first microseconds too, from 3.1 on. Block 0 to block 3 did land at that rate ((1.05 x 3 + 1.84) MB in 14.7 us, 338 KB/us). But group 0's 1.84 MB took from 3.1 to 11.8, 211 KB/us, though GpSimd was held until 7 us, and block 0 came 3.9 us behind it, where 1.05 MB are 3.1. A row that showed it was there: group 0 took until 13.62 in [rows 3]. By the forecast's own steps behind the landing, 30.5 + 16.6 puts group 2's first gate matmul at 47.1; it came at 48.1 on the median core. So 3.4 of the 4.4 us that are missing are the landing. The other 1.0 is TensorE's own: it did not wait for block 3 at all, but for block 1, and ran 11 to 16 matmuls at 0.373 us, which the forecast priced at 0.189; the 0.238 mean of the first 32 ([rows 3], 7.63 us) already held those at 0.373.
- **The ends of the start.** The end named for "only the first byte", -3.9, was still too good; block 3 came 0.2 us earlier, and blocks 0 and 1 as well. The prediction named first blocks that land no earlier than before as a sign of its being wrong; 0.2 us is all that speaks against that sign. The Trainium skill's rule on shared engines ("DMA: Bandwidth & Descriptors", Issuing engines are not separate DMA queues) was right in that another queue brought no more bandwidth. What was won is TensorE's order of blocks (1.8 of 2.1).
- **Projections: the mechanism right.** -1.8 for -2.8 on the median core, -1.2 and what is left, -0.6, for -1.4 twice. The wait for the clearing of `Vb` came (2.25 us), and TensorE's waits behind it make 1.9 us (0.94, 0.74 and 0.26), as forecast, though in other places. The terms were read on core 0, where the projections took 119.96 us before; there -2.9 came for the -2.8.
- **Attention: right in size, wrong in its split.** -4.0 for -4.9 at the median, -6.1 on core 0, from which the terms were read. Outputs and tile were summed as -3.0 (with the bank) and -1.9; they only work together.
- **Mix output: wrong side of an overlap.** -4.9 for -3.8. GpSimd's adds took 1.04 us beside products, not 1.43, since they mostly started first; the row it was priced by [rows 5] has the add start second. The rival "fully locked out" fell for the same reason, and came true in part in the two kernels with group 0 on GpSimd's queue (adds of 1.37, one wait of 0.7 us).
- **Tail: right**, -1.0 for -0.7, read from the two traces alone.
- **The slower rival** did not come, for the reason given against it. Where it was forced it cost 39.6 us for the formula's 26.
- **The landing in the range owes something to luck.** Errors of +4.4, +1.0, +0.9, -1.1 and -0.3 us make +4.9 on a median core. The slowest core, against which the sum was made, gave 2.4 of that back: core 0 had been 2.1 us above the median in attention and 1.2 in the projections, and lost both. That 1435.5 is also the time of the rival "only the first byte" is chance, since its term for the start, -3.9, did not come either.

No version tried beats the changed kernel: the best, with blocks 0 and 1 apart, takes 1435.33 us, which can't be told from it.

## What to carry to other kernels

A rate read in the middle of a load stream says nothing of its first microseconds; add up what has landed by the first time it is needed, and compare that with all bytes ahead of it. Where two engines slow each other down, ask which one starts first in each pair, and which one has slack; a chain that never pauses can start second each time and go on paying. Before tenths of a microsecond are read as a gain, look how far executions with the same code there lie apart: 0.9 us at this kernel's start. And read a term on all cores before summing it: the time is the slowest core's, so a stage whose length differs between cores is worth more than its median.

## What the hardware showed unexpectedly

- Pieces on SP's queue, issued first, landed 4 to 6 us apart beside GpSimd's loads, and 1.5 to 2.3 apart when GpSimd's were held until the first had landed; that wait was worth 7.5 us.
- After an idle start 8 to 16 gate matmuls ran at 0.373 us each (1.2 GHz) with the granted clock at 1.00; with zero matmuls ahead they ran at 0.189, but on five of eight cores seven to nine matmuls at 0.373 came back behind later pauses (0.76 us at 26.4 and 0.35 at 28.5 on core 0), while on core 4 none did behind pauses of 2.26 and 1.60.
- A start 0.3 us later turned a chain of GpSimd's adds from 1.04 us each to 1.37: of an add and a VectorE product that started within 0.4 us of each other, the first kept its time and the second took 0.17 to 0.76 us more.
